# Three modulation chunks moved from VectorE to rows on TensorE, and the other three to later head slots

## The reference, cut to what matters

```
c_act = silu(c)
mod = c_act @ ada_w[0] + ada_b[0]            # 1024 x 6144: 12 chunks of 512 columns
sh_a, sc_a, gt_a, sh_m, sc_m, gt_m = split(mod, 6)
h = rms_norm(x) * (1 + sc_a) + sh_a           # chunks 0 to 3
x = x + gt_a * diff_attention(h)              # chunks 4, 5
h = rms_norm(x) * (1 + sc_m) + sh_m           # chunks 6, 7 (shift), 8, 9 (scale)
x = x + gt_m * mlp(h)                         # chunks 10, 11
```

## Time and profile before

| | us |
|---|---|
| median of 3 runs | 1349.8 |
| lowest, highest | 1344.44, 1352.47 |
| the profiled execution | 1349.93 |
| its span, first to last instruction | 1348.1 |
| TensorE busy in the span | 1284.0 (95%) |
| VectorE busy | 884.5 (66%) |
| ScalarE busy | 683.4 (51%) |

### The profile page before, as it was taken

The page is one execution under the profiler, slowest core; times in us unless marked ns, Lnnn a source line. Parts: engine busy times, 40 slices in busy tenths (PEclk is TensorE's granted clock), DMA queues, the critical chain, the costliest instruction groups (busy, mean ns, idle before and its releaser), DMA issues.

```text
span 1348.1 us, 21994 instructions
## 1 busy us (share of the span) xinstructions
PE 1284.0 (95%) x8460; PEld 1111.7 (82%) x8460; DVE 884.5 (66%) x1589; ACT 683.4 (51%) x1196; POOL 140.6 (10%) x166
## 2 busy tenths in 40 slices
PE   6889899999999999999999889999999999999999
PEld 2778789889879846799998776798998787898997
DVE  3479788999768577776555776656555566655453
ACT  2536454444554456555454684654444666654542
POOL 0112111100100000011010130011010110010100
PEclk8979899999999999999999999999999999999999
DMA  9996539899868533278555351396556464466650
GB/s 350 343 293 217 176 116 328 306 336 345 312 190 226 185 112 115 70 249 298 188 175 150 113 173 47 107 330 180 184 172 183 129 203 126 152 188 188 189 158 32
DMA packets 144776, 267.42 MB, mean 198 GB/s; under 512 B 11040, under 2 KB 50208, under 8 KB 144288
## 3 DMA queue, kind: packets, MB, share of 16 engines
q1 hardware_dynamic: 138592, 250.94, 57.6%
q0 software_dynamic: 3456, 12.58, 2.9%
q10 hardware_dynamic: 2624, 2.49, 0.6%
HBM read 264.83 MB, written 1.15 MB: 197 GB/s over the span
## 4 chain that ended last, share of the span: by engine, by line
PE 71%; DVE 12%; issue 6%; DMA 5%; ACT 3%; POOL 1%; SPq 1%; DVEq 0%; ACTq 0%; POOLq 0%
PE bank L544 14%; PE bank L546 13%; PE bank L545 13%; PE ps_s L544 4%; PE ps_s L545 4%; PE ps_s L546 4%; PE ps_p L546 4%; PE ps_p L545 4%; PE ps_p L544 4%; DVE wlo L1617 3%; DMA xn<-in_ada_w 2%; DVE acc L1636 2%; DMA wring<-in_mlp_w 2%; DVE acc L1665 1%; ACT whi L2776 1%
## 5 line engine op out<-in xcount | busy, mean ns | idle before, releaser
L1617 DVE TENSOR_TENSOR wlo<-wring,whi 128x1024 fp32r<-128x1024 f32 (+1 forms) x376 | 454.1, 1217 | 254.4 <-ACT whi L2776 251.3
L2776 ACT ACTIVATE whi<-wring 128x1024 fp32r<-128x1024 f32 (+1 forms) x376 | 388.6, 1045 | 374.3 <-PE bank L546 137.8
L544 PE MATMUL bank<-h_hi,whi 128*128 128x256 f32 (+1 forms) x1224 | 351.0, 287 | 4.3 <-DVE wlo L1617 1.9
L545 PE MATMUL bank<-h_lo,whi 128*128 128x256 f32 (+1 forms) x1224 | 347.7, 284 | 0.0
L546 PE MATMUL bank<-h_hi,wlo 128*128 128x256 f32 (+1 forms) x1224 | 347.5, 284 | 0.0
L544 PEld LDWEIGHTS bank<-h_hi,whi 128*128 128x128 f32 (+1 forms) x1224 | 235.6, 192 | 9.3 <-issue 6.4
L545 PEld LDWEIGHTS bank<-h_lo,whi 128*128 128x128 f32 (+1 forms) x1224 | 235.7, 193 | 0.7
L546 PEld LDWEIGHTS bank<-h_hi,wlo 128*128 128x128 f32 (+1 forms) x1224 | 235.7, 193 | 0.0
L3436 POOL TENSOR_TENSOR ex<-ex 128x512 f32<-128x512 f32 x64 | 78.1, 1223 | 683.1 <-ACT g_hi L2907 683.1
L544 PE MATMUL ps_s<-whi,g_hi 128*128 128x512 f32 x256 | 101.6, 397 | 1.3 <-DVE wlo L1617 1.3
L544 PE MATMUL bank<-whi,h_hi 128*128 128x512 f32 (+2 forms) x232 | 92.0, 396 | 9.3 <-DVE wlo L1617 2.8
(11 more groups left out here) (398 smaller groups left out, 1832.9 us busy)
## 6 DMA issues: line engine op xcount, KB each, us to landing
wring<-in_mlp_w SPq DMA_DIRECT2D x128, 512.0 KB, 4.9
wring<-in_ada_w SPq DMA_DIRECT2D x72, 512.0 KB, 7.6
wring<-in_mlp_w_in SPq DMA_DIRECT2D x64, 512.0 KB, 3.9
wring<-in_mlp_w_out SPq DMA_DIRECT2D x64, 512.0 KB, 4.2
wring<-in_a_w_in SPq DMA_DIRECT2D x24, 512.0 KB, 10.6
xn<-in_ada_w POOLq DMA_DIRECT2D x24, 512.0 KB, 5.1
wring<-in_moba_w_qkv SPq DMA_DIRECT2D x24, 512.0 KB, 3.9
wring<-in_kv_ada_w SPq DMA_DIRECT2D x16, 512.0 KB, 8.3
```

The lines of the kernel that those rows point to most:

```text
L544: nc.tensor.matmul(out, lh, rh, start=first, stop=False, skip_group_check=mixed)
L545: nc.tensor.matmul(out, lh, rl, start=False, stop=False, skip_group_check=mixed)
L1617: v.tensor_tensor(piece_view(wlo, p), raw_view(p), piece_view(whi, p).bitcast(F32), ALU.subtract).then_inc(lo_ready, 1)
L2776: a.activation(piece_view(whi, p), raw_view(p), ACT.Copy).then_inc(hi_ready, 1)
```

## The change

`MOD_SLOTS` becomes `(4,)`, `CHUNKS` becomes `(4, 5, 8)`, and `ROWS = (9, 6, 7)` names the three that move. Each of these takes four loads of 512 KB in the ring of SyncE, behind the weights of head 7 and mixed with the first six pieces of `a_out`. In slots 5, 6 and 7 TensorE makes one of them with `late_rows`, and ScalarE drains it to `acc`. `sum_columns` adds up chunks 5 and 9 in slot 6, and chunks 6, 7 and 8 behind slot 7; `sum_drain` adds their biases. VectorE keeps 12 steps instead of 24: none before slot 2, two at the end of slot 2 behind `diff_combine`, two in each of slots 3 to 7, none afterwards. GpSimd issues its first loads only when the scores of head 0 have been made. ScalarE instead of VectorE copies `gate_row` in slot 7.

```diff
-MOD_SLOTS = (0, 2, 4, 6)
-CHUNKS = (4, 5, 8, 9, 6, 7)
+MOD_SLOTS = (4,)
+CHUNKS = (4, 5, 8)
+ROWS = (9, 6, 7)
...
-    plan += [c[:4] + (c[4][:3],) for c in a_out]
+    first_six = [c[:4] + (c[4][j:j + 1],) for c in a_out for j in range(3)]
+    for i, c in enumerate(ROWS):
+        plan += ada(0, (c,)) + first_six[2 * i:2 * i + 2]
...
-        late = ada_order[22:26]
+        late = [ada_order[c] for c in ROWS] + ada_order[22:26]
...
+            def sum_columns(use, rows, sources, chunks):
+
+                for i in rows:
+                    bank_emptied(pe, ("late_rows", i))
+                pe.wait_ge(matvec_done, chunks)
+                b = bank_take(pe, use)
+                piece_of[use] = -1
+                for n, i in enumerate(sources):
+                    for j in range(4):
+                        last = nc.tensor.matmul(bank[:, b, 4 * n + j:4 * n + j + 1], acc[:, i, j * P:(j + 1) * P],
+                                                ones[:, 0:1], start=True, stop=True)
+                last.then_inc(filled[b], 1)
+
             for s in range(8):
...
                 qk_piece(s, b, 1)
+                if s == 6:
+                    sum_columns("rows_a", [0], [1, 0], 2)
+                if s >= 5:
+                    late_rows(s - 5)
                 if s == 7:
                     gate_rows("a0", 16)
...
-            mod_columns(matvec_order[4])
+            sum_columns("rows_b", [1, 2], [1, 0, 2], 3)
...
             diff_back(7)
-            pe.wait_ge(matvec_done, 6)
-            pe.wait_ge(sem("diff_evened"), 1)
-            for j in range(4):
-                last = nc.tensor.matmul(early_banks[0][:, j:j + 1], acc[:, 2, j * P:(j + 1) * P], ones[:, 0:1],
-                                        start=True, stop=True)
-            last.then_inc(sem("early_columns"), 1)
...
-            keep_ahead("dve", 7, 1)
-            for j in range(4):
-                chunk_step(j)
-                keep_ahead("dve", 8 + j // 2, 1)
+            for j in range(3):
+                keep_ahead("dve", 7 + j, 1)
             dve.wait_ge(sem("bias_in"), 16)
             for s in range(8):
...
+                if s == 7:
+                    sum_drain("rows_a", (CHUNKS[1], ROWS[0]))
                 if slot_head(s - 1) is not None:
                     diff_scores(slot_head(s - 1))
                 if slot_head(s - 3) is not None:
                     diff_even(slot_head(s - 3))
-                for i in range(2):
-                    chunk_step(4 + 2 * s + i)
-                    keep_ahead("dve", p + 1)
+                if s >= 3:
+                    chunk_step(2 * s - 4)
+                keep_ahead("dve", p + 1)
+                if s >= 3:
+                    chunk_step(2 * s - 3)
                 if slot_head(s - 1) is not None:
                     diff_combine(slot_head(s - 1))
+                if s == 2:
+                    chunk_step(0)
+                    chunk_step(1)
                 if slot_head(s - 3) is not None:
                     diff_low(slot_head(s - 3))
-                if s == 7:
-                    gate("a0")
...
-            mod_drain(matvec_order[4])
             diff_scores(7)
             diff_even(5)
-            chunk_step(20)
+            sum_drain("rows_b", (ROWS[1], ROWS[2], CHUNKS[2]))
...
-            chunk_step(21)
...
-            chunk_step(22)
...
-            chunk_step(23)
...
+                if s >= 5:
+                    late_sums(s - 5, acc[:, (s - 5) % 2, :])
+                if s == 7:
+                    for g in range(2):
+                        drain(("a0", "gate", g), gate_row[:, g * W:(g + 1) * W], (0, W))
...
                 if k == rstd_at[("diff", 0)]:
-                    pool.wait_ge(sem("a0_split"), 6)
-                    for n in range(12):
+                    pool.wait_ge(sem("diff_scored"), 1)
+                    for n in range(4):
                         chunk_load(n)
                 roots(k)
-                if rstd_at[("diff", 0)] <= k < rstd_at[("diff", 6)]:
-                    n = 12 + 2 * (k - rstd_at[("diff", 0)])
+                if rstd_at[("diff", 0)] <= k < rstd_at[("diff", 4)]:
+                    n = 4 + 2 * (k - rstd_at[("diff", 0)])
```

More of the change, by code:

```diff
@@ L430, in build @@
         matvec_order = [ada_order[c] for c in CHUNKS] + ada_order[10:22] + ada_order[26:28]
-        drain_order = [ada_order[c] for c in opening + CHUNKS] + ada_order[10:]
+        drain_order = [ada_order[c] for c in opening + CHUNKS[:2] + ROWS + CHUNKS[2:]] + ada_order[10:]
         def drained_by(*chunks):
@@ L636, in gate_rows @@
                                                 ident[:, :], start=True, stop=True)
+                    if name == "a0":
+                        piece_of[name, "gate", g] = -1
                     last.then_inc(filled[b], 1)
@@ L720, in late_rows @@
                 b = bank_take(pe, ("late_rows", i)) if k0 == 0 else uses["late_rows", i][0]
-                if i < 2:
+                if i < 5:
                     piece_of["late_rows", i] = -1
@@ L740, in late_columns @@
                 for i in rows:
-                    bank_emptied(pe, ("late_rows", i))
+                    bank_emptied(pe, ("late_rows", 3 + i))
                 b = bank_take(pe, ("late_mod", pair))
@@ L1046, in _ @@
             mlp("m0", ada_order[10:22], lambda: gate_rows("m0", 40), inside=turn_inside)
-            late_rows(0)
-            late_rows(1)
+            late_rows(3)
+            late_rows(4)
             turn_scaled("kv", 1)
@@ L1260, in between @@
                 elif b < 8:
-                    late_rows(b // 2, 4 * (b % 2) + 2 * i, 4 * (b % 2) + 2 * i + 2)
+                    late_rows(3 + b // 2, 4 * (b % 2) + 2 * i, 4 * (b % 2) + 2 * i + 2)
                 elif b < 18:
@@ L1671, in chunk_step, with sum_drain @@
                     v.memset(stat[:, 1:2], 0.0).then_inc(matvec_done, 1)
[L1673 to L1679, removed]
+            def sum_drain(use, chunks):
+                src = bank_full(dve, use)
+                for i, c in enumerate(chunks):
+                    at = col["ada_b0"] + 4 * c
+                    ins = v.tensor_tensor(mod[:, 4 * c:4 * c + 4], src[:, 4 * i:4 * i + 4], params[:, at:at + 4], ALU.add)
+                    if i < len(chunks) - 1:
+                        link(ins)
+                ins.then_inc(drained[uses[use][0]], 1)
+                bank_emptied(dve, use)
+                v.memset(stat[:, 1:2], 0.0).then_inc(mod_drained, len(chunks))
             def rstd(width, n, tag=None, eps=None):
@@ L2193, in _ @@
             diff_low(7)
-            last_drain()
             gain(gs, "mn0", 32)
@@ L2987, in _, with late_sums @@
             act.wait_ge(sem("subln_ready"), 1)
+            def late_sums(i, to):
+                key = ("late_rows", i)
+                a.activation(to, bank_full(act, key), ACT.Copy).then_inc(drained[uses[key][0]], 1)
             for s in range(8):
@@ L3017, in _ @@
             mlp("m0")
-            def late_sums(i):
-                key = ("late_rows", i)
-                a.activation(row_sums[i], bank_full(act, key), ACT.Copy).then_inc(drained[uses[key][0]], 1)
             last = last_of(("m0_w2", 7))
-            scaled_norm("kv", (hk_hi, hk_lo, gs2, mod[:, 48:56]), 4, 4096, last - 3, last, late_sums)
+            scaled_norm("kv", (hk_hi, hk_lo, gs2, mod[:, 48:56]), 4, 4096, last - 3, last,
+                        lambda t: late_sums(3 + t, row_sums[t]))
             for t in range(TT):
@@ L3106, in _ @@
                 if b in (5, 7):
-                    late_sums((b - 1) // 2)
+                    late_sums(3 + (b - 1) // 2, row_sums[(b - 1) // 2])
                 if b == 6:
```

## The result

The changed kernel takes **1340.1 us**, the median of 19 runs (1337.38 to 1347.0). The kernel before, timed beside it in another 19, takes 1347.22 (1344.22 to 1353.45). The ratio is 0.9947, with a 95% interval of 0.9937 to 0.9958: faster by 0.53%, or 7.1 us. The forecast was 1339.4, from a gain of 10.5.

A forecast was written before the change was run, and what follows sets the result against it. Head slots bound by TensorE and VectorE loops of 8.9 us, the front by chunk steps waiting for loads on VectorE. Front gains 12.5, slots from 4 give back 2.0, tail nothing: 1349.93 less 10.5 is 1339.4 us; range 1335 to 1346.

The forecast's parts named there:

- Front: Slots 0 to 3: without chunk steps before slot 2's end, head 3's scores start at 96.7 instead of 109.21, gaining 12.5 us.
- At 4.6 us it just fits: Chunk load 2, issued at 86.0 for a step at 90.5, arrives in time; the longest landing, 8.0, costs 3.4 us.
- later loads have a whole slot of 8.9: Chunk loads after load 2 each have 8.9 us to land before their step.
- rival (b): Bytes bound the front: full DMA engines keep head weights late, gain only 1.8 to 4 us, 1346 to 1348; chance 0.12.
- I take half of that 1.5: Slot 4: TensorE's waits in slot 3 slow the clock behind them; half of 1.5 us charged, slot 5's scores at 106.3.
- Slots 5 and 6: TensorE's loop is longer: 8.10 plus 1.82 per row chunk gives 9.9; adding up two chunks, 1.75 more, gives 11.7 us.
- the rule weighed there: Row matmuls: four column groups overlap, so four cost near one; set aside for the measured 0.91 us per four.
- Slot 7: Slot 7's to head 7's scores: scores, rows, gate, mixing, three sums, first `a_out` piece and turning take 14.1 us, to 142.0.
- my sign of being wrong: Slots 5 to 7 above 10, 12 and 14 us would mean a wrong row price or a late drain.
- Rival (a): Chunk loads or the clock eat a part: gain 4 to 9 us, about 1343; chance 0.22.
- (c): Steps starve in slots 3 to 7 if loads land slower than the 8.9 us loop: slower, 1357 at 12.4 us; chance 0.05.
- (d): More than forecast: no slow clock in slot 4 or from 159.83, gain 12.5 us or more, 1336; chance 0.06.

The follow-up runs named there:

- the gate on VectorE: Changed kernel with the two gate copies moved back from ScalarE to VectorE at the end of slot 7: 1339.55 us, 0.9941 of the kernel before.
- the wait filled: Changed kernel plus 13 unread identity matmuls before the turning of head 2, where TensorE stood 3.21 us: 1338.74 us, 0.9929 of the kernel before.
- the front alone: Kernel before with no chunk step before slot 2's end, all 24 on VectorE, twelve behind slot 7, no rows: 1363.58 us, 1.0122 of before.
- row chunks twice: Changed kernel with the 16 matmul instructions of each of the three row chunks issued twice: 1346.95 us, 0.9994 of the kernel before.
- sums in the wait: Changed kernel with chunks 6, 7 and 8 added up ahead of the third `a_out` piece, not in slot 7: 1338.58 us, 0.9937 of before.
- the twelve steps at the front: Changed kernel with VectorE's twelve steps and their loads back where the first twelve stood before, none later: 1349.64 us, 1.0001 of the kernel before.
- the steps in the gaps: Changed kernel with steps 0 and 1 done one each in slots 1 and 2, before the second split, loads earlier: 1335.91 us, 0.9909 of before.

## Why the prediction came out as it did

The kind, the place and the mechanism were right: the time is inside the range, and 0.7 us from the forecast. That nearness is luck, for the gain is not as near: I forecast 10.5 and 7.1 came. The absolute time fits so well because the three runs I had of before had a median of 1349.8, and 19 runs have 1347.22. By the forecast gain the 19 runs would have given 1336.7.

**Front, 12.5 forecast, 11.85 measured.** Of this, 0.77 is that slot 0 began earlier, which no term had. Counted from the start of slot 0, head 3's scores were forecast at 34.9 us and came at 36.3: 1.4 late. The chain through slots 0 to 2 was right to 0.3 us on that count: heads 0 and 1 turned without a wait, and the maxima of head 2 came at 26.8 where 27.0 was forecast. In slot 3 I had waits of about 1 and about 2 us; they measured 0.83 and 3.21, and the load that was 1.56 us late accounts for the excess. "At 4.6 us it just fits" was said of load 2. That one fitted, with at most 4.2 us; load 3 did not. The step that failed is "later loads have a whole slot of 8.9": load 3 goes out behind step 1 and had only 5.4 us (86.92 to 92.35), and it took 7.0, the price of the busy stretch and not the 4.6. The DMA share was 0.76 while it ran (86.9 to 94), little above the 0.70 of the earlier trace rows, so a full DMA is not shown to be the cause; a weight load of SyncE went out beside it at 87.90. The Trainium skill, DMA: Bandwidth & Descriptors, section Issuing engines are not separate DMA queues, says that loads of both engines run on the same 16 DMA engines, which would fit. But rival (b), which went by it, fell: the head weights came in time.

**Slot 4, 9.6 forecast, 10.41 measured,** 11.42 in the trace with the gate on VectorE, 8.91 with the wait filled. "I take half of that 1.5" is a term that was too small. The row I took it from the earlier trace rows had it: 1.5 after a wait of 1.90. Here the wait was 3.21 and the cost 1.50 to 2.51, all of it. It varies: behind a wait of 2.32 (the front alone) slot 4 took 8.91, nothing extra; behind 2.49 (row chunks twice) 10.08; behind 2.60 (sums in the wait) 11.34. The third `a_out` piece shows the same scatter with one and the same wait, 2.43 to 2.50 us: from it to the fourth piece 13.8 us pass in four traces (the twelve steps at the front, the row chunks twice, the wait filled, the gate on VectorE), and 15.2 to 15.3 in three (before, after, the steps in the gaps). What decides it is not known.

**Slots 5 and 6, 9.9 and 11.7 forecast, 10.02 and 11.69 measured.** A row chunk costs 1.85 (113.54 - 111.69), where 1.82 was taken from the earlier trace rows, and doubled it costs about the same again. The two summed chunks cost 1.77 for 1.75. That column groups overlap, as the rule weighed there has it, the trace shows too. All row instructions, and their durations (lowest, median, highest, in ns):

```profile
L733 PE MATMUL bank<-wring,pos_f x48: 592/592/617, 111.7 to 134.7; 128*32 128x512 f32 x48
```

A run of four of them, one per column group, lasts 0.61 us from its first start to its last end (125.68 in the trace with the gate on VectorE), where one alone lasts 0.59: they start together. So the price of 1.85 for 16 already has the overlap in it.

**Slot 7, 14.1 forecast, 15.94 measured,** and 14.42 in four other traces (the twelve steps at the front, the wait filled, the steps in the gaps, the gate on VectorE). So the terms missed 0.3, and this execution added 1.5 by the clock at 0.53. This is my sign of being wrong, slots above 10, 12 and 14, but neither of the causes that I gave it: the rows kept their price and no drain was late. I take the 1.5 for a matter of this execution.

**From head 7's scores to the third piece, 7.32 forecast, 7.23 measured,** and nothing gained by the end of steps 20 to 23, as said. With twelve steps at the front, and the same short tail, it is 7.21.

In the profiled execution these make up the 3.4 missing from 10.5: front 0.65, slot 4 0.81, slots 5 and 6 0.11, slot 7 1.84, together 3.41 (the front's 0.65 is net of the 0.77 that came as a gift). Rival (a), loads or clock eating a part, is what happened in small; its 1343 was too much, since the rows kept their price. Rivals (c) and (d) did not come: no load took over 8.5 us.

**Behind the MLP's start.** Of the lead of 7.2 us at 181 the profiled execution kept 3.3. It lost the rest where the two kernels do the same work: one matmul group stands at 481.79 against 490.23, 8.4 ahead, and a later one at 539.39 against 542.80, 3.4 ahead. Between them, from 470 to 500 us, its clock was 0.83 and that of before 1.00; the run with steps in the gaps also shows 1.00 there. Other traces of edited kernels have 0.83 (the wait filled) and 0.94 (the gate on VectorE). No edit touches that stretch, so I take it for a difference between executions; what sets the clock off there I have not tested. These 5.0 and the 1.5 of slot 7 are nearly the 6.9 us by which this execution lies above the median of its runs; that is an inference from one trace. Why the lead had grown from 7.2 to 8.4 before that, I have not traced.

**What stays open.** The two traces agree with the medians at the MLP's start (7.2 and 7.1), but partly by chance. With the twelve steps at the front the median equals that of before, and yet that trace has the MLP 2.0 earlier (186.46 against 188.48). Of these 2.0, 1.4 is the clock behind the third `a_out` piece (15.2 against 13.8 us to the fourth). The profiled execution of before had that slow stretch, as that of after had it and 1.5 in slot 7 besides; which is the usual case for either kernel, one trace each does not tell. How the 3.4 divide between load and clock over many executions is not settled by one trace of each.

## What to carry to other kernels

A stall before a late engine is often a matter of order on it: here 12 optional steps stood, in program order, ahead of the work that TensorE waited for, and moving them behind it gave the gain, while taking as many off the engine gave none without that. Work so postponed must still end in time; its other half has to find another engine, or the kernel may get slower (1.2% here, with the one placing tried). When loads are chained to steps, check every load of the chain against its own use, at the landing time of the busy stretch, and count what a wait of TensorE costs in clock behind it: here 1.5 to 2.5 us for one of 3.2, and anything from nothing to 2.4 for one of 2.3 to 2.6.

## What was not expected of the hardware

TensorE's clock fell to its lower level while TensorE was not idle. In the profiled execution of after this happened at 141.9, 45 us after its last wait, behind rows, gate, turning back, mixes and the 24 instructions that add up three chunks (133.39 to 140.62), 1.3 us behind the last of them; with the sums in the wait it happened some 1 us behind the 24 one-column instructions, in both traces that have them there (146.23 and 140.48). In the five other traces the same instructions in slot 7 did not do it. I have not isolated what in them counts.

A one-column matmul costs TensorE some 0.11 us per instruction (24 in 2.6: 138.02 to 140.62), twice for each float32 product, although it yields one column; adding up three chunks costs more than making one of them as rows (2.6 against 1.85). At the lower clock the same 24 took 5.28 (the front alone). Executions of one kernel differ by 10 us (1337.38 to 1347.0), and traces of kernels with the same work there by a clock of 0.83 against 1.00 over 30 us: a difference of a few us between two profiled executions says nothing before it is seen where they differ.
